# Second half of a transformer layer on TensorE: the up product by seven products over half of its depth

## The chip, the cores and the metric

The kernel runs on one core of a Trainium2 chip. The metric is the device time of one execution in microseconds (us); lower is better. The engines are TensorE (PE), VectorE (DVE), ScalarE (ACT), GpSimd (POOL) and SyncE (SP), which here issues transfers only. They run side by side and wait for one another on semaphores.

## The reference

One layer for 1024 prompt tokens and 64 sample tokens (1088 columns in all), everything in fp32. Width 1024, D_FF 4096. The change lies in the last two lines of the layer:

```
x = x + merged @ w_out
f = rmsnorm(x, norm2_w) @ w_up              # (tokens, 1024) @ (1024, 4096)
x = x + jnp.square(jax.nn.relu(f)) @ w_down  # (tokens, 4096) @ (4096, 1024)
```

A final RMSNorm follows. Ahead of it lie the input projection, a gated convolution, attention for both token groups, and two projections; they are the same in both kernels.

## The kernel before

**Products in three parts.** To keep fp32 accuracy with fp32r matmuls, every operand is split into a high part (a cast to fp32r) and a low part (the operand less its high part). A product is three matmuls into one bank of PSUM: high by high, high by low, low by high (`product`, line 1301). A matmul takes a 128 x 128 stationary tile and up to 512 moving columns.

**Normalised activations.** After the output projection, blocks of 128 tokens are normalised, turned on PE (event `turn_y`, line 1684), and written as `yh` (ScalarE, line 1931) and `yl` (VectorE, line 2312): eight depth tiles (128 rows of the depth 1024) by 1088 columns.

**Twins.** D_FF is worked through in 16 twins; twin n holds the up tiles 2n and 2n+1, each 128 of the 4096 rows. For each up tile, three chunks of columns (384, 384 and 320) are computed, 8 depth tiles by 3 matmuls each (event `up`). VectorE takes relu into `hf`, ScalarE squares it in place. GpSimd splits each up tile's weights (`tail_tile`: cast at line 1229, subtraction at line 1232).

**Seven products down.** The down product of a twin, a 256-deep product for 1024 tokens and 1024 outputs, is already done by the Strassen-Winograd scheme: seven products of half the size (event `prod`, lines 1641 to 1643: 7 x 12 matmuls of 512 columns), with sums of activations on VectorE (event `sum`, line 2335), their high parts on ScalarE and low parts on VectorE (event `prep`, lines 1953 and 2343), and sums of weights (`tw`) with their split on GpSimd (`down_op`, lines 1247 to 1261). The results are added onto `x1` by VectorE (`add_pair`, line 2269). The sample tokens go apart in 8 matmuls (event `few`, lines 1652 and 1653).

**What sets the order.** It is written out by hand: the list `tail` (from line 722) names events, and every engine walks the same list and does its share. For twin n from 1 to 15 it is: sums of twin n-1, six `up` chunks of twin n with `relu` and one or two `prep` of twin n-1 beside each, then the seven `prod` and two `few` of twin n-1. GpSimd has an order of its own: for each twin, five down operands, an up tile, three down operands, an up tile. Down operands go through a ring of five places (`d_hi`, `d_lo`); an operand waits until the one five before it has been used for the last time. At the end, the last twin's down product is done plainly in blocks with the final norm, and GpSimd makes its operands between the last down operands (`end_low`).

## Time and profile before

| | us |
|---|---|
| three runs | 1613.03, 1613.94, 1614.47 |
| median | 1613.94 |
| the profiled execution | 1613.12 |
| its span | 1611.4 |
| up and down stage, from the first up matmul to the last down product | 884.0 to 1581 |

The profiled execution's time is 1.7 us above its span, which runs from the first to the last instruction. PE is busy for 1600.1 us of it, VectorE for 1057.3, GpSimd for 725.1 and ScalarE for 533.8.

A row of a timeline gives start, duration, engine, line of the kernel, operation, output and inputs, shape, count, and in brackets the idle time ahead and what ended it. Matmuls overlap in the array: a duration there is longer than the distance to the next start, and the distance is what PE spends. A row of groups gives after the bar the busy time and the mean in ns of one, then the idle time ahead.

### The profile page before, as it was taken

To read this page: it belongs to the slowest core of one execution; us is meant where nothing else is said; L and a number is where in the kernel's file an instruction comes from. 1 tells how busy PE (TensorE), PEld (TensorE's weight loads), DVE (VectorE), ACT (ScalarE), POOL (GpSimd) and SP (SyncE) were. 2 spreads that over 40 slices of the span, in tenths; PEclk is the share of its full clock that TensorE was granted. 3 is DMA by queue.
4 is the path that set the end of the run, shared out by engine and by line. 5 is a ranking of instruction groups with operands and counts; after the bars stand their busy time and mean duration, and the time that the engine had idled before them with its cause. 6 is when DMAs were issued, how large, how long until landed. Compare 5 with 4: busy or idle time off the path is not lost.

```text
span 1611.4 us, 25421 instructions
## 1 busy us (share of the span) xinstructions
PE 1600.1 (99%) x9776; PEld 1482.7 (92%) x9776; DVE 1057.3 (66%) x1408; ACT 533.8 (33%) x1047; POOL 725.1 (45%) x597
## 2 busy tenths in 40 slices
PE   9999999999999999999999999999999999999998
PEld 8999999999998888999988989999999999999996
DVE  7685877859712221356433588777778888877777
ACT  6655665556522221432134411111111111111124
POOL 5212121121212111223587486666666776666653
PEclk9999999999999999999999999999999999999999
DMA  4201112011184767372354111110111111111012
GB/s 165 68 27 55 54 40 69 27 41 55 41 281 149 234 222 231 117 244 96 129 186 144 58 53 52 53 42 16 49 53 53 52 53 53 53 53 51 18 51 111
DMA packets 133491, 144.99 MB, mean 90 GB/s; under 512 B 7839, under 2 KB 98619, under 8 KB 133372
## 3 DMA queue, kind: packets, MB, share of 16 engines
...
q14 instruction: 41, 0.34, 0.1%
q10 hardware_dynamic: 146, 0.04, 0.0%
...
## 4 chain that ended last, share of the span: by engine, by line
PE 87%; DVE 8%; ACT 3%; issue 1%; DVEq 0%; ACTq 0%
PE ps L1307 51%; PE ps L1641 6%; PE ps L1642 6%; PE ps L1643 6%; DVE sp L2140 2%; PE ps L1598 2%; PE ps L1603 2%; PE ps L1601 2%; PE ps L1501 2%; DVE zc L2132 1%; PE ps L1457 1%; PE ps L1467 1%; PE ps L1545 1%; PE ps L1513 1%; ACT sp L1815 1%
## 5 line engine op out<-in xcount | busy, mean ns | idle before, releaser
L1307 PE MATMUL ps<-xh,wh 128*128 128x352 f32 (+1 forms) x956 | 322.3, 337 | 0.9 <-DVE xl L2113 0.7
L1307 PE MATMUL ps<-xh,wl 128*128 128x352 f32 (+1 forms) x956 | 312.5, 327 | 0.0
L1307 PE MATMUL ps<-xl,wh 128*128 128x352 f32 (+1 forms) x956 | 312.2, 327 | 0.0
L2269 DVE TENSOR_TENSOR x<-ps,x 128x1024 f32<-128x1024 f32 x210 | 257.1, 1225 | 42.9 <-PE ps L1643 24.5
L1150 POOL CAST wh<-raw 128x1024 fp32r<-128x1024 f32 x48 | 50.4, 1050 | 477.6 <-issue 213.2
L1307 PE MATMUL ps<-yh,wh 128*128 128x384 f32 (+1 forms) x768 | 250.5, 326 | 0.0
L1307 PE MATMUL ps<-yh,wl 128*128 128x384 f32 (+1 forms) x768 | 250.5, 326 | 0.0
L1307 PE MATMUL ps<-yl,wh 128*128 128x384 f32 (+1 forms) x768 | 250.2, 326 | 0.0
L1939 ACT ACTIVATE hf<-hf 128x384 f32<-128x384 f32 (+1 forms) x96 | 48.6, 508 | 554.9 <-DVE hf L2322 554.9
L1307 PEld LDWEIGHTS ps<-xh,wh 128*128 128x128 f32 x956 | 179.8, 188 | 17.2 <-issue 15.5
L1307 PEld LDWEIGHTS ps<-xl,wh 128*128 128x128 f32 x956 | 180.0, 188 | 0.7
L1307 PEld LDWEIGHTS ps<-xh,wl 128*128 128x128 f32 x956 | 179.5, 188 | 0.0
L1641 PE MATMUL ps<-d_hi,a_hi 128*128 128x512 f32 x420 | 163.7, 390 | 0.3 <-DVE x L2257 0.3
L1643 PE MATMUL ps<-d_lo,a_hi 128*128 128x512 f32 x420 | 163.7, 390 | 0.0
L1642 PE MATMUL ps<-d_hi,a_lo 128*128 128x512 f32 x420 | 163.7, 390 | 0.0
L1159 POOL TENSOR_TENSOR wl<-raw,wh 128x1024 fp32r<-128x1024 f32 x48 | 116.2, 2420 | 97.0 <-DVE zc L2142 91.2
L1307 PEld LDWEIGHTS ps<-yh,wh 128*128 128x128 f32 x768 | 144.2, 188 | 0.7 <-POOL wl L1232 0.2
L1307 PEld LDWEIGHTS ps<-yl,wh 128*128 128x128 f32 x768 | 144.2, 188 | 0.5
L1307 PEld LDWEIGHTS ps<-yh,wl 128*128 128x128 f32 x768 | 144.1, 188 | 0.0
L1232 POOL TENSOR_TENSOR wl<-raw,wh 128x1024 fp32r<-128x1024 f32 x56 | 135.5, 2420 | 10.1 <-POOL wh L1229 10.1
L1259 POOL CAST d_hi<-raw_d 128x512 fp32r<-128x512 f32 x60 | 37.5, 624 | 166.0 <-PE ps L1653 141.6
L2184 DVE COPY kct<-ps 128x512 f32<-128x512 f32 x32 | 22.1, 692 | 128.2 <-PE ps L1501 103.8
...
## 6 DMA issues: line engine op xcount, KB each, us to landing
...
```

The costliest lines, as they stand in the source:

```text
L1150: g.tensor_copy(wh[s][:, :], raw[s][:, :]).then_inc(w_hi, 1)
L1159: g.tensor_tensor(wl[s][:, :], raw[s][:, :], f32(wh[s][:, :]), ALU.subtract).then_inc(w_split, 1)
L1232: g.tensor_tensor(low[:, :], raw[n % 3][:, :], f32(high[:, :]), ALU.subtract).then_inc(w_split, 1)
L1259: g.tensor_copy(high, src).then_inc(d_hi, 1)
L1307: ins = mm(out, lhs[:, k * P:(k + 1) * P], rhs[:, x], start=(first and a == 0 and m == 0), stop=(last and a == n - 1 and m == 2))
L1501: ins = tr(bank(tb, p * P, (p + 1) * P), cache[g][:, (a * NPAIR + p) * P:(a * NPAIR + p + 1) * P], ident[:, :])
L1598: mm(out, hi, w, start=k == 0, stop=False)
L1641: mm(out, a_hi[p][:, x], w, start=not onto, stop=False, skip_group_check=onto)
L1642: mm(out, a_lo[p][:, x], w, start=False, stop=False, skip_group_check=onto)
L1643: ins = mm(out, a_hi[p][:, x], lo_w, start=False, stop=True, skip_group_check=onto)
L1939: A(x, x, ACT.Square).then_inc(hf_made, 1)
L2269: V_.tensor_tensor(x, src, x, ALU.add).then_inc(step_free, 1)
```

## The change

The up product of twins 1 to 15 is done in another way. Its output is two up tiles (i = 0, 1) by two halves of the prompt tokens (j = 0, 1), its depth eight tiles. The first four depth tiles are done by seven products in the Strassen-Winograd scheme, the last four plainly.

- PE does eight entries `mix` per twin: seven products of 6 matmuls (two depth tiles by three), and four plain sums of 12 matmuls, which share the entries (`MIX`: bank, product, plain part). All have 512 columns: 90 matmuls. Four banks hold partial sums that the scheme uses more than once; PE goes on adding onto a bank once a copy has been kept.
- ScalarE copies such partial sums into `hf` (`keep`), VectorE adds them to another bank (`join`), ScalarE does relu and square, which were one instruction on each.
- The 64 sample tokens have 16 matmuls of 256 columns with the weights as moving side, a copy (`few_move`) and a ninth entry of two small matmuls in plain fp32 that turn and add their high and low parts.
- The weights of a twin are one buffer `raw_u` (two loads of 4 depth tiles). Six operands are made of it: four plain ones of two depth tiles, whose cast is on ScalarE (`u_cast`) and whose subtraction is on GpSimd, and two of sums (`twist` on 256 columns), with cast and subtraction on GpSimd. They share the ring of five places with the eight down operands; places are handed out by who is free first.
- GpSimd's order per twin is six up operands, then eight down operands.
- In the first twin (still plain), the activations lie in other buffers, so the second and third chunks are cut in pieces at columns 512 and 1024; VectorE writes plain copies `y_plain` in `turn_y`, and VectorE and ScalarE make four sums of them (`twist`, `twist_low`) during its last chunks.

The core of the diff:

```diff
+        MIX_BANK = {"x": 4, "y": 5, "z": 6, "w": 0, "few": 1}
+        MIX = [("x", 0, None), ("y", 1, (0, 0)), ("z", 3, None), ("x", 2, None), ("z", 5, (0, 1)), ("x", 4, None), ("w", 6, (1, 0)),
+               ("x", None, (1, 1))]
+        KEEP = {0: (0, 0), 2: (1, 1), 3: (0, 1), 5: (1, 0)}
+        JOIN = {1: (0, 0), 4: (0, 1), 6: (1, 0), 7: (1, 1)}
+        U_KT = (0, 4, 6, 2)
+        PLAIN_AT = {f: (x, (f - U_KT[x]) * 2 * P) for x in range(4) for f in (U_KT[x], U_KT[x] + 1)}
+        W_AT = {p: [(PLAIN_AT[f][0], PLAIN_AT[f][1] + i * P) for f in fs] for p, i, fs in ((0, 0, (0, 1)), (1, 0, (2, 3)), (6, 1, (2, 3)))}
+        W_AT.update({p: [(x, (KQ * h + q) * P) for q in range(KQ)] for p, x, h in ((3, 4, 0), (2, 4, 1), (5, 5, 0), (4, 5, 1))})
+        U_LAST = (1, 7, 7, 6, 3, 5)
...
         for n in range(1, N_TWIN):
-            tail += [("sum", n - 1, k) for k in range(4)]
-            todo = list(PREP)
-            for m in range(6):
-                e = 2 * n + m // 3, m % 3
-                tail += [("up", *e), ("relu", *e)]
-                for _ in range(BESIDE_UP[m]):
-                    tail.append(("prep", n - 1, todo.pop(0)))
-            assert not todo
+            m = n - 1
+            if n == 1:
+                tail += [("u_cast", n, x) for x in range(4)]
+            tail += [("sum", m, 0), ("sum", m, 1), ("mix", n, 0), ("keep", n, 0), ("prep", m, 0), ("prep", m, "few0"), ("prep", m, "few1"),
+                     ("prep", m, 1), ("prep", m, 6), ("prep", m, 3), ("prep", m, 4), ("mix", n, 1), ("few_move", n), ("sum", m, 2),
+                     ("mix", n, 2), ("keep", n, 2), ("mix", n, 3), ("keep", n, 3), ("prep", m, 2), ("join", n, 1), ("sum", m, 3),
+                     ("mix", n, 4), ("mix", n, 8), ("prep", m, 5), ("mix", n, 5), ("keep", n, 5), ("join", n, 4), ("join", n, 8),
+                     ("mix", n, 6), ("join", n, 6), ("mix", n, 7), ("join", n, 7)]
             if n == LAST_TWIN:
                 tail.append(("end_prep",))
             tail += [("prod", n - 1, 0), ("few", n - 1, 0)]
             tail += [("prod", n - 1, p) for p in range(1, N_WAY)]
+            if n < LAST_TWIN:
+                tail += [("u_cast", n + 1, x) for x in range(3)]
             tail.append(("few", n - 1, 1))
+            if n < LAST_TWIN:
+                tail.append(("u_cast", n + 1, 3))
...
+        RING = []
+        for n in range(1, N_TWIN):
+            RING += [("u", n, x) for x in range(len(U_LAST))]
+            RING += [("d", n - 1, k) for k in range(N_OP)]
+        ring_no = {e: g for g, e in enumerate(RING)}
+
         def op_used(g):
 
-            n, k = divmod(g, N_OP)
-            return done_no[(OP_LAST[k][0], n, *OP_LAST[k][1:])]
+            kind, n, k = RING[g]
+            return done_no["mix", n, U_LAST[k]] if kind == "u" else done_no[(OP_LAST[k][0], n, *OP_LAST[k][1:])]
+
+        slot_of, slot_after = [], []
+        free_at = [tile_end["up", 0], tile_end["up", 0], tile_end["up", 1], tile_end["up", 1], tile_end["up", 1] + 1]
+        for g in range(len(RING)):
+            slot_of.append(free_at.index(min(free_at)))
+            slot_after.append(min(free_at))
+            free_at[slot_of[g]] = op_used(g)
...
+            def load_pair(n):
+
+                if n == 1:
+                    sp_.wait_ge(w_split, 6 * NPAIR + 3 * KT + 2 + N_OUT + 2)
+                else:
+                    sp_.wait_ge(d_lo, ring_no["u", n - 1, len(U_LAST) - 1] + 1)
+                apart(sp_)
+                for s in range(2):
+                    sp_.dma_start(blocks(raw_u, 2 * P)[:, 4 * s:4 * s + 4, :], wup[:, 4 * s:4 * s + 4, ds(2 * n * P, 2 * P)]).then_inc(u_in, 16)
...
+            def slot_free(of):
+
+                pool.wait_ge(step_done, slot_after[of])
+                if of == TOP_FIRST:
+                    pool.wait_ge(twist_lo, 4)
+                apart(pool)
+
+            def split_op(of, src):
+
+                high, low = w_hi_at[slot_of[of]][:, :], w_lo_at[slot_of[of]][:, :]
+                kind, n, x = RING[of]
+                if kind == "u" and x < 4:
+                    pool.wait_ge(u_hi, 4 * (n - 1) + x + 1)
+                else:
+                    g.tensor_copy(high, src).then_inc(d_hi, 1)
+                    pool.wait_ge(d_hi, of + 1 - 4 * n if kind == "u" else of + 1 - 4 * (n + 1))
+                g.tensor_tensor(low, src, f32(high), ALU.subtract).then_inc(d_lo, 1)
+                pool.wait_ge(d_lo, of + 1)
+
+            def up_op(n, x):
+
+                rows_ = blocks(raw_u, 2 * P)
+                a11, a12, a21, a22 = (rows_[:, KQ * j:KQ * j + KQ, i * P:i * P + P] for i in range(2) for j in range(2))
+                s1, s2, s4, s3 = (blocks(tw[t])[:, KQ * h:KQ * h + KQ, :] for t in range(2) for h in range(2))
+                of = ring_no["u", n, x]
+                if x == 0:
+                    pool.wait_ge(u_in, 32 * n)
+                if x < 4:
+                    slot_free(of)
+                    split_op(of, raw_u[:, U_KT[x] * 2 * P:(U_KT[x] + 2) * 2 * P])
+                elif x == 4:
+                    twist(s1, a21, a22, ALU.add)
+                    twist(s2, s1, a11, ALU.subtract)
+                    slot_free(of)
+                    split_op(of, tw[0][:, :])
+                else:
+                    twist(s3, a11, a21, ALU.subtract)
+                    twist(s4, a12, s2, ALU.subtract)
+                    slot_free(of)
+                    split_op(of, tw[1][:, :])
...
+                for x in range(len(U_LAST)):
+                    up_op(n + 1, x)
+                for k in range(N_OP):
+                    if n == LAST_TWIN - 1 and k >= N_SOON:
                         end_low(k - N_SOON)
                     down_op(n, k)
...
+                    if m < len(MIX):
+                        where, p, over = MIX[m]
+                        out = bank(MIX_BANK[where])
+                        if m in (3, 4, 5, 7):
+                            pe.wait_ge(kept, 4 * (n - 1) + KEPT_FOR[m])
+                        else:
+                            pe.wait_ge(step_free, mix_bank_read(n, m))
+                        begun = where == "x" and m > 0 or (where == "z" and m > 2)
+                        if over:
+                            i, j = over
+                            for f in range(KT // 2, KT):
+                                x, at = PLAIN_AT[f]
+                                pe.wait_ge(d_lo, ring_no["u", n, x] + 1)
+                                ins = three(out, weight(x, at + i * P), [y_at(f, part, j * HS, (j + 1) * HS) for part in range(2)],
+                                            not begun and f == KT // 2, p is None and f == KT - 1)
+                            begun = True
+                        if p is not None:
+                            pe.wait_ge(d_lo, ring_no["u", n, W_AT[p][0][0]] + 1)
+                            if n == 1 and p in TWIST_NO:
+                                pe.wait_ge(twist_lo, TWIST_NO[p] + 1)
+                            for q in range(KQ):
+                                ins = three(out, weight(*W_AT[p][q]), [y_op[p][part][:, q * HS:(q + 1) * HS] for part in range(2)],
+                                            not begun and q == 0, q == KQ - 1)
+                        if m == 1:
+                            pe.wait_ge(d_lo, ring_no["u", n, 3] + 1)
+                            order_ = [f for x in (1, 2, 3, 0) for f in (U_KT[x], U_KT[x] + 1)]
+                            for f in order_:
+                                x, at = PLAIN_AT[f]
+                                y = y_few[f // (KT // 2)][:, f % (KT // 2) * P:f % (KT // 2) * P + P]
+                                for t, w in enumerate((w_hi_at, w_lo_at)):
+                                    ins = mm(bank(MIX_BANK["few"], 0, 2 * P), y, w[ring("u", n, x)][:, at:at + 2 * P],
+                                             start=f == order_[0] and t == 0, stop=f == order_[-1] and t == 1)
...
+                elif e[0] == "twist":
+                    act.wait_ge(step_done, tile_end["up", 0])
+                    for k, p in enumerate(TWIST_OF):
+                        if k == 3:
+                            act.wait_ge(step_done, tile_end["up", 1])
+                        act.wait_ge(twisted, k + 1)
+                        A(y_op[p][0][:, :], y_plain[TWIST_IN[k]][:, :], ACT.Copy).then_inc(twist_hi, 1)
...
+                elif e[0] == "u_cast":
+                    _, n, x = e
+                    of = ring_no["u", n, x]
+                    act.wait_ge(u_in, 32 * n)
+                    act.wait_ge(step_done, slot_after[of])
+                    assert of != TOP_FIRST
+                    A(w_hi_at[slot_of[of]][:, :], raw_u[:, U_KT[x] * 2 * P:(U_KT[x] + 2) * 2 * P], ACT.Copy).then_inc(u_hi, 1)
...
+                elif e[0] == "keep":
+                    _, n, m = e
+                    i, j = KEEP[m]
+                    if n >= 2 and m == 0:
+                        act.wait_ge(op_lo, len(PREP) * (n - 1))
+                    act.wait_ge(step_done, done_no["mix", n, m])
+                    A(hf[n % 2][i][:, j * HS:(j + 1) * HS], bank(MIX_BANK[MIX[m][0]]), ACT.Copy).then_inc(kept, 1)
+                elif e[0] == "join":
+                    _, n, m = e
+                    act.wait_ge(step_free, read_no["mix", n, m])
+                    parts = [hf[n % 2][JOIN[m][0]][:, JOIN[m][1] * HS:(JOIN[m][1] + 1) * HS]] if m < 8 else [hf[n % 2][i][:, SEQ:NTOK] for i in range(2)]
+                    for x in parts:
+                        if m < 8:
+                            A(x, x, ACT.Relu).then_inc(relu_made, 1)
+                            act.wait_ge(relu_made, 4 * (n - 1) + RELU_NO[m])
+                        A(x, x, ACT.Square).then_inc(hf_made, 1)
...
+                        if f < KT // 2 and b < NB:
+                            x = (f % KQ) * HS + b * P % HS
+                            V_.tensor_scalar(y_plain[f // KQ, b * P // HS][:, x:x + P], src, w2c[:, f:f + 1], None, ALU.mult)
...
+                elif e[0] == "join":
+                    _, n, m = e
+                    v.wait_ge(step_done, done_no["mix", n, m])
+                    if m < 8:
+                        i, j = JOIN[m]
+                        x = hf[n % 2][i][:, j * HS:(j + 1) * HS]
+                        v.wait_ge(kept, 4 * (n - 1) + 1 + [KEEP[k] for k in (0, 2, 3, 5)].index(JOIN[m]))
+                        V_.tensor_tensor(x, bank(MIX_BANK[MIX[m][0]]), x, ALU.add).then_inc(step_free, 1)
```

On GpSimd (POOL), around the beginning of a steady twin, the order before was (`raw` and `wh`, `wl`: an up tile and its parts; `raw_d`: down weights, `tw`: their sums, `d_hi`, `d_lo`: places of the ring):

```order
L1229 CAST wh_61<-raw_59 128x1024 [waits step_done,d_lo,raw_in0]
L1232 TENSOR_TENSOR wl_63<-raw_59,wh_61 128x1024 [waits w_hi]
L1259 CAST d_hi_116<-raw_d_127 128x512 [waits step_done]
L1261 TENSOR_TENSOR d_lo_121<-raw_d_127,d_hi_116 128x512 [waits d_hi]
L1255 TENSOR_TENSOR tw_129<-raw_d_127,tw_129 128x512 [waits d_lo,step_done]
L1259 CAST d_hi_117<-tw_129 128x512 [waits t_made]
L1261 TENSOR_TENSOR d_lo_122<-tw_129,d_hi_117 128x512 [waits d_hi]
L1259 CAST d_hi_118<-raw_d_126 128x512 [waits d_lo,step_done]
L1261 TENSOR_TENSOR d_lo_123<-raw_d_126,d_hi_118 128x512 [waits d_hi]
L1229 CAST wh_62<-raw_60 128x1024 [waits step_done,d_lo,raw_in1]
L1232 TENSOR_TENSOR wl_64<-raw_60,wh_62 128x1024 [waits w_hi]
```

and is now, from the subtraction of the first up operand of a twin to the second operand of sums:

```order
L1344 TENSOR_TENSOR d_lo_149<-raw_u,d_hi_144 128x512 [waits step_done,d_lo,u_in,u_hi]
L1344 TENSOR_TENSOR d_lo_150<-raw_u,d_hi_145 128x512 [waits d_lo,step_done,u_hi]
L1344 TENSOR_TENSOR d_lo_148<-raw_u,d_hi_143 128x512 [waits d_lo,step_done,u_hi]
L1344 TENSOR_TENSOR d_lo_151<-raw_u,d_hi_146 128x512 [waits d_lo,step_done,u_hi]
L1324 TENSOR_TENSOR tw_138<-raw_u 128x256 [waits d_lo]
L1324 TENSOR_TENSOR tw_138<-tw_138,raw_u 128x256 [waits t_made]
L1342 CAST d_hi_147<-tw_138 128x512 [waits t_made,step_done]
L1344 TENSOR_TENSOR d_lo_152<-tw_138,d_hi_147 128x512 [waits d_hi]
L1324 TENSOR_TENSOR tw_139<-raw_u 128x256 [waits d_lo]
L1324 TENSOR_TENSOR tw_139<-raw_u,tw_138 128x256 [waits t_made]
L1342 CAST d_hi_144<-tw_139 128x512 [waits t_made,step_done]
L1344 TENSOR_TENSOR d_lo_149<-tw_139,d_hi_144 128x512 [waits d_hi]
```

All splits of up weights now stand in one run ahead of the down operands, in pieces of 512 columns; the third subtraction waits (through its cast) for the last of the seven products of the twin before, the fourth and the cast of the first sum operand for the `few` behind it.

On ScalarE (ACT), where the first twin ends and twin 1 begins, the order is now (`y_plain` to `yh`: casts of the four sums of activations; `hf<-hf`: squares of the first twin; `d_hi<-raw_u`: casts of up weights; the last row is the first kept copy):

```order
L2122 ACTIVATE yh_97<-y_plain_105 128x1024 [waits twisted,step_done]
L2122 ACTIVATE yh_101<-y_plain_107 128x1024 [waits twisted]
L2122 ACTIVATE yh_99<-y_plain_108 128x1024 [waits twisted]
L2122 ACTIVATE yh_103<-y_plain_106 128x1024 [waits twisted,step_done]
L2115 ACTIVATE hf_1_135<-hf_1_135 128x320 [waits step_free]
L2115 ACTIVATE hf_0_134<-hf_0_134 128x384 [waits step_free]
L2115 ACTIVATE hf_1_135<-hf_1_135 128x384 [waits step_free]
L2129 ACTIVATE d_hi_143<-raw_u 128x512 [waits step_done,u_in]
L2129 ACTIVATE d_hi_144<-raw_u 128x512 [waits step_done,u_in]
L2129 ACTIVATE d_hi_145<-raw_u 128x512 [waits step_done,u_in]
L2129 ACTIVATE d_hi_146<-raw_u 128x512 [waits step_done,u_in]
L2142 ACTIVATE hf_0_136<-ps 128x512 [waits step_done]
```

Before, only the squares stood there. The fourth cast waits for the last matmul of the first twin, and the casts of weights stand behind it.

## Rows read from the trace of the kernel before

**Rows 1.** The page: PE's busy time, and the clock in 40 slices.
```profile
PE 1600.1 (99%) x9776; PEld 1482.7 (92%) x9776; DVE 1057.3 (66%) x1408; ACT 533.8 (33%) x1047; POOL 725.1 (45%) x597
...
PEclk9999999999999999999999999999999999999999
```

**Rows 2.** Timeline of PE: end of a twin, up part, down products, next twin.
```profile
1045.09 0.39 PE L1653 MATMUL ps<-d_lo,few 128*128 128x512 f32 x1
1045.32 0.33 PE L1307 MATMUL ps<-yh,wh 128*128 128x384 f32 x1
...
1069.04 0.39 PE L1641 MATMUL ps<-d_hi,a_hi 128*128 128x512 f32 x1
...
1089.95 0.33 PE L1307 MATMUL ps<-yh,wh 128*128 128x384 f32 x1
```

**Rows 3.** Timeline of PE in the attention stage: matmuls of 256, 128, 64 columns.
```profile
241.57 0.28 PE L1484 MATMUL ps<-tl,vhl 128*128 128x256 f32 x1
241.69 0.22 PE L1483 MATMUL ps<-th,vhl 128*128 128x128 f32 x1
241.75 0.28 PE L1484 MATMUL ps<-tl,vhl 128*128 128x128 f32 x1
...
487.62 0.43 PE L1520 MATMUL ps<-ks,qblk 128*32 128x64 f32 x16
```

**Rows 4.** Groups by line: the first from the page, the others of the last stages.
```profile
L1232 POOL TENSOR_TENSOR wl<-raw,wh 128x1024 fp32r<-128x1024 f32 x56 | 135.5, 2420 | 10.1 <-POOL wh L1229 10.1
...
L1261 POOL TENSOR_TENSOR d_lo<-raw_d,d_hi 128x512 fp32r<-128x512 f32 x60 | 78.0, 1300 | 4.8
...
L1259 POOL CAST d_hi<-raw_d 128x512 fp32r<-128x512 f32 x60 | 37.5, 624 | 166.0 <-PE ps L1653 141.6 <-DMA raw_d<-in_w_down 13.2 <-PE ps L1643 5.6
...
L1953 ACT ACTIVATE a_hi<-sum 128x512 fp32r<-128x512 f32 x60 | 35.5, 615 | 0.0
L1939 ACT ACTIVATE hf<-hf 128x384 f32<-128x384 f32 x64 | 33.6, 526 | 502.4 <-DVE hf L2322 502.4
...
L1961 ACT ACTIVATE end_wh<-end_raw 128x1024 fp32r<-128x1024 f32 x2 | 2.0, 1051 | 1.7 <-DMA end_raw<-in_w_down 1.7
```

**Rows 5.** Timeline of GpSimd and VectorE where the same twin begins.
```profile
1047.44 1.62 POOL L1249 TENSOR_TENSOR tw<-raw_d,tw 128x512 f32<-128x512 f32 x1
...
1045.75 0.68 DVE L2257 TENSOR_TENSOR x<-ps,x 128x512 f32<-128x512 f32 x1
1046.35 1.56 DVE L2335 TENSOR_TENSOR sum<-hf,hf 128x512 f32<-128x512 f32 x1
...
1062.57 0.68 DVE L2343 TENSOR_TENSOR a_lo<-sum,a_hi 128x512 fp32r<-128x512 f32 x1
```

**Rows 6.** Timeline of PE and VectorE: last chunks of the first twin.
```profile
902.41 0.34 PE L1307 MATMUL ps<-yh,wh 128*128 128x384 f32 x1
...
910.73 0.33 PE L1307 MATMUL ps<-yh,wh 128*128 128x384 f32 x1
...
900.27 2.16 DVE L2312 SCALAR_TENSOR_TENSOR yl<-ps,cols,yh 128x128 fp32r<-128x128 f32 x8 [1.98 <-ACT yh L1931]
```

**Rows 7.** Timeline of GpSimd and PE: last down products.
```profile
1562.52 2.42 POOL L1268 TENSOR_TENSOR end_l<-hf,end_h 128x1024 fp32r<-128x1024 f32 x1 [13.68 <-ACT end_h L1958]
...
1578.17 1.30 POOL L1261 TENSOR_TENSOR d_lo<-raw_d,d_hi 128x512 fp32r<-128x512 f32 x1
...
1559.95 0.39 PE L1641 MATMUL ps<-d_hi,a_hi 128*128 128x512 f32 x1
...
1579.94 0.39 PE L1652 MATMUL ps<-d_hi,few 128*128 128x512 f32 x1
```

**Rows 8.** Timeline of PE in the first down products.
```profile
940.05 0.50 PE L1641 MATMUL ps<-d_hi,a_hi 128*128 128x512 f32 x1 [0.30 <-DVE x L2257]
```

**Rows 9.** Windows at the span's end: length, busy times, then the clock.
```profile
1605.00:1607.50 2.50, 0.00 (x0) 0.00 (x0) 2.43 (x6) 1.67 (x4) 0.00 (x0) 1.00 0.34 143
1607.50:1609.00 1.50, 0.00 (x0) 0.00 (x0) 0.83 (x2) 0.00 (x0) 0.00 (x0) 0.62 1.01 415
```

263 lines of the change are left out of this document (169 added, 94 removed).

## The prediction

> **What bounds the kernel now.** I read the page first, for which engine is full. TensorE is busy in 99% of the span, its clock is at full level in every slice [rows 1]. Nothing but work on PE can be worth much, and any new wait of PE is paid in full. I then read PE's timeline over one twin in steady state, for where such a twin begins and ends. From the first matmul of its up part to the first of the down products are 23.72 us, and from there to the next twin 20.91 us [rows 2]. That is 144 and 92 matmuls, one after the other without a hole; the 92 matmuls of 512 columns go at 0.2273 us each, the chunks of 384 columns at 0.1733 (48 of them in 8.32 us [rows 6]). There are fifteen such twins, 44.63 us each. The other engines have to be ahead of PE, no more. Last I read GpSimd and VectorE in the same twin, for what their instructions cost alone and beside each other [rows 4, 5], because the change gives both a longer list ahead of PE.
>
> **1. The arithmetic of a twin.** The 144 matmuls go. In their place stand 90 of 512 columns: seven products of 6, and four plain sums of 12. By 0.2273 that is 20.46 us. The 64 sample tokens go apart, as 16 matmuls of 256 columns. A 256-column matmul lies 0.12 us before the next [rows 3]: 1.92 us. The two small matmuls with plain fp32 operands are four passes. Sixteen such passes over 32 weight columns fit in 0.43 us [rows 3], under 0.03 each; a 256-column pass is 0.12. So four cost between 0.1 and 0.5 us; I take 0.45, for they load all 128 columns and PE drains between kinds. Together 22.83 against 23.72: **0.89 us less, times 15: -13.4 us** (-12.7 to -18.6). The saved sixteenth of the product is smaller than it sounds because the gain of wide chunks is partly spent on the sample tokens.
>
> **2. The fifth operand, in every steady twin.** The third entry of a twin (product 3) needs the operand of sums s1 and s2. Its place in the ring is free only when the last matmul of the twin before is done, and so is that of the operand before it. The chain from there, at time 0: a waiting engine starts 0.43 us later (VectorE's add at 1045.75, PE having gone on at 1045.32 [rows 2, 5]); ScalarE's cast 0.6; GpSimd's subtraction 1.3 and 0.2 to the next; two sums of 256 columns, 0.73 each (estimate from 1.30 for 512 and 2.42 for 1024 columns), a cast 0.62, a subtraction 1.30 [rows 4]; 0.1 for each of five hand-overs. Sum 6.4. PE wants it after 24 matmuls of 512 and 16 of 256, at 7.4. Alone it would be in time by 1.0 us. But VectorE does its two sums and three low parts just then. Where it meets GpSimd both wait: a sum began at 1046.35 and took 1.56 us, against 0.68 for the same work at 1062.57, and GpSimd's subtraction beside it 1.62 against 1.30 [rows 4, 5]. So each of the five adds some 0.3 to the chain, 1.5 in all: ready at 7.9, **0.45 us late, 14 times: +6.3 us**. The lower bound is no wait (interference under 1.0), the upper that each adds its own whole length, three of 0.68 and two of 0.23, and starts ahead: 1.45 late, +20.3. I take the value near the measured rows. The Trainium skill (SBUF — State Buffer, the shared port pair) says that the pair is locked for a whole instruction and the loser blocks fully; by that alone the sum would be the upper bound, while the rows show a growth of 0.32 for GpSimd.
>
> **3. The start.** At the end of the first twin, PE now finds no operand. Before, GpSimd split the next tiles meanwhile and PE went straight on at 910.73 [rows 6]. Now ScalarE stands in the order: cast of the fourth twist (waits for that last matmul), three squares, then the casts for twin 1. From the last matmul: 0.43, 1.05, 3 x 0.45 (squares chained), 0.6 and 0.1, that is 3.5 [rows 4]. GpSimd then does four subtractions (1.3 + 0.2 each, 6.0), two sums (1.6), a cast (0.7), a subtraction (1.3): 12.9 to 13.1, plus six meetings with VectorE of 0.3: 14.9. PE's own work up to product 3 is 7.4. **+7.6 us** (5.8 with no meeting, 9.9 with whole lengths), of which some 5 lie ahead of twin 1 and the rest in it. The load of up weights for twin 1 waits for a split that ends around the first chunk of the first twin, so it costs nothing; the down weights' load waits for the last twist but is used 20 us later.
>
> **4. The first twin in pieces.** Two chunks out of three are cut at columns 512 and 1024: 36 more matmuls for each tile. A 128-column one follows at 0.06 us [rows 3], a 64-column one costs no less than a third of that and no more than the same. So 24 extra of 64 columns cost 0.3 to 1.0, 12 of 128 0.2; per tile 0.85, twice: 1.7. VectorE also writes a plain copy: four more instructions of about 0.27 for the last block [rows 6], and the chunk waits for all of it: 0.6. **+2.3 us** (1.0 to 3.5). The same copies in the output projection lie under PE work of 4 us a tile and cost nothing; were they late there, each of eight blocks would show its 1 us.
>
> **5. The end.** In the last twin GpSimd's run of end splits is already the tightest: it starts at 1562.52, ends with the split of 1578.17 (1.30 us), and PE uses that at 1579.94, 20.0 us after its products began at 1559.95 [rows 7]. The chain of 17.0 us keeps its length. But two down operands that were made early now wait for ring places that the up part frees at its very end, and stand ahead of it: 0.43 + 2.1 + 1.5 + 2.1, so it starts 6.3 us after the products' start, ends at 23.3. **+3.4 us** (2.4 to 4.0), and all behind it follows.
>
> **6. What goes.** A 0.3 us wait of the first down products on VectorE [rows 8], whose sums GpSimd then slowed: **-0.3**. ScalarE's casts, copies and squares (some 25 of 0.6 in 44) have room. The copy that the last plain sum waits for stands behind a high part that waits for VectorE's sum; by the same steps it is done 2.8 us early, so it costs nothing unless VectorE falls behind by that.
>
> Sum: -13.4 + 6.3 + 7.6 + 2.3 + 3.4 - 0.3 = +5.9. The profiled execution took 1613.12, which gives 1619.0. The median of the runs is 0.8 above it, so the forecast is **1619.5 us**.
>
> **Rivals.** *GpSimd is in time in every steady twin.* Decides: interference under 1.0 us instead of 1.5, so if VectorE's small low parts slip through. Then term 2 is nothing: 1613.2, no change; with the lower ends of terms 1, 3, 4 and 5 too (-2 to -5 for the small matmuls, -1.8, -1.3, -1.0) it is 1607 to 1609, faster. For it: only 1.0 us has to be found, and GpSimd's ordinary subtractions average 1.30 even beside VectorE [rows 4]. Against: the sums stand exactly there. *The lock counts in full*, which is the rule cited above: 1.45 us per twin, 1633. *The clock falls at the start.* After its last matmul, in the profile's last microseconds, PE stood still; the clock was full in 1605 to 1607.5 and lower in the next stretch [rows 9], 1.2 instead of 2.4 GHz. PE will stand still some 5 us here. At half clock the 7.4 us up to product 3 become 14.8, of which 2.6 fit into its wait: 0 to 5 us, 1622. The Trainium skill (TensorE: Matmul & The Clock Gate, HAM oscillation) warns of such holes before matmuls. *VectorE and ScalarE trail*: the last kept copy comes 1 us late in each twin, 1634. That the seven products save nothing is excluded by the count.
>
> **Chances.** Forecast 0.40, in time 0.36, full lock 0.13, clock 0.07, trailing 0.04. A measurement of this kernel tells 0.2%, 3.2 us, from no change: 1610.7 to 1617.2 around the median. Of the forecast 0.07 falls in there, of the rival in time 0.16, its other 0.20 below. So faster 0.20, same 0.23, slower 0.57. The likeliest case alone has 1614 to 1625. The range of 1607 to 1630 leaves out 0.05 below and 0.13 above.
>
> **What would show it.** In the changed profile: about 22.8 us of PE work between products plus a hole of some 0.5 us ahead of product 3 that GpSimd's low part of a twist ends; a hole of about 5 us after the first twin, ended by GpSimd, and more before product 3; one of 3 us before the last sample-token product. If the hole before product 3 is missing in the steady twins, term 2 is wrong and the kernel is no slower. If holes stand before the last plain sum instead, ScalarE's queue is the fault.

## The result and the profile after

| | before | after |
|---|---|---|
| median of four runs | 1613.9 | 1634.73 |
| range | 1613.03 to 1614.47 | 1633.04 to 1635.15 |
| the profiled execution | 1613.12 | 1633.04 |
| its span | 1611.4 | 1631.3 |

The changed kernel is **1.3% slower**: the ratio is 1.0128, with a 95% interval of 1.0110 to 1.0145. The forecast was 1619.5, its range ended at 1630. The side was right, the size was not. Between the two profiled spans lie 19.9 us, between the two medians 20.8.

The page and the waits of PE come first, as before the change. The columns of the waits are: what waited and for what; us in total, times, longest.

```profile
PE 1599.0 (98%) x9338; PEld 1425.3 (87%) x9338; DVE 1040.3 (64%) x1448; ACT 649.4 (40%) x1246; POOL 819.3 (50%) x718
...
PE ps L1828 <- POOL d_lo L1344: 17.9, 15, 4.3
PE ps L1773 <- POOL d_lo L1344: 3.5, 1, 3.5
```

PE has 438 matmuls less than in [rows 1] and is busy for 1.1 us less. Against that stand sixteen waits that were not there, 21.4 us in all. Each is ended by GpSimd: one in each of the fifteen twins, and one at the end.

**The steady twin.** PE's timeline, with the first row of each part (compare [rows 2]); then GpSimd and VectorE in the same twin, and ScalarE's two casts. The product in question is product 3, the third entry.

```profile
1056.57 0.39 PE L1828 MATMUL ps<-yh,d_hi 128*128 128x512 f32 x1
...
1062.01 0.28 PE L1866 MATMUL ps<-d_hi,y_few 128*128 128x256 f32 x1
...
1065.04 0.47 PE L1828 MATMUL ps<-yh,d_hi 128*128 128x512 f32 x1 [0.97 <-POOL d_lo L1344]
...
1080.60 0.39 PE L1763 MATMUL ps<-d_hi,a_hi 128*128 128x512 f32 x1
...
1101.47 0.39 PE L1828 MATMUL ps<-yh,d_hi 128*128 128x512 f32 x1
```

```profile
1056.63 1.30 POOL L1344 TENSOR_TENSOR d_lo<-raw_u,d_hi 128x512 fp32r<-128x512 f32 x1 [3.11 <-ACT d_hi L2129]
1058.14 1.50 POOL L1344 TENSOR_TENSOR d_lo<-raw_u,d_hi 128x512 fp32r<-128x512 f32 x1 [0.20 <-PE ps L1828]
1059.72 1.07 POOL L1324 TENSOR_TENSOR tw<-raw_u 128x256 f32<-128x256 f32 x1
1060.87 1.07 POOL L1324 TENSOR_TENSOR tw<-tw,raw_u 128x256 f32<-128x256 f32 x1
1062.13 1.10 POOL L1342 CAST d_hi<-tw 128x512 fp32r<-128x512 f32 x1 [0.19 <-POOL tw L1324]
1063.30 1.59 POOL L1344 TENSOR_TENSOR d_lo<-tw,d_hi 128x512 fp32r<-128x512 f32 x1
...
1057.60 0.88 DVE L2579 TENSOR_TENSOR sum<-hf,hf 128x512 f32<-128x512 f32 x1
1058.41 1.78 DVE L2579 TENSOR_TENSOR sum<-hf 128x512 f32<-128x512 f32 x1
1060.11 1.22 DVE L2587 TENSOR_TENSOR a_lo<-hf,a_hi 128x512 fp32r<-128x512 f32 x1
...
1062.08 0.68 DVE L2587 TENSOR_TENSOR a_lo<-hf,a_hi 128x512 fp32r<-128x512 f32 x1
...
1062.68 1.09 DVE L2587 TENSOR_TENSOR a_lo<-hf,a_hi 128x512 fp32r<-128x512 f32 x1
...
1055.92 0.63 ACT L2129 ACTIVATE d_hi<-raw_u 128x512 fp32r<-128x512 f32 x1 [4.81 <-PE ps L1765]
1056.83 0.63 ACT L2129 ACTIVATE d_hi<-raw_u 128x512 fp32r<-128x512 f32 x1 [0.28 <-PE ps L1774]
```

The up part lasts 24.03 us here and the twin 44.90, against 23.72 and 44.63. The sixteen matmuls of 256 columns end at 1063.90 (1.89 us after 1062.01), and PE goes on at 1065.04: a hole of 1.14, and the first matmul behind it takes 0.09 more than its 0.23. Without these 1.23 us the twin would take 43.67, less than before. The operand was due 7.33 us after the twin's start and was finished at 8.32. GpSimd began with the fourth operand at 1.57, because the third, whose ring place came free only with the seventh down product, was still under way. And every one of its five instructions is longer than its length alone: VectorE is at work beside each.

**The start.** The end of the first twin and the start of the next, on PE, ScalarE and GpSimd; then windows (length, PE busy, clock, DMA share, GB/s).

```profile
915.90 0.28 PE L1819 MATMUL ps<-yh,wl 128*128 128x256 f32 x1
920.47 0.76 PE L1828 MATMUL ps<-yh,d_hi 128*128 128x512 f32 x1 [4.29 <-POOL d_lo L1344]
...
917.18 1.28 ACT L2115 ACTIVATE hf<-hf 128x320 f32<-128x320 f32 x3
918.37 2.17 ACT L2129 ACTIVATE d_hi<-raw_u 128x512 fp32r<-128x512 f32 x4
...
919.06 1.26 POOL L1344 TENSOR_TENSOR d_lo<-raw_u,d_hi 128x512 fp32r<-128x512 f32 x1 [30.89 <-ACT d_hi L2129]
...
928.03 1.62 POOL L1344 TENSOR_TENSOR d_lo<-tw,d_hi 128x512 fp32r<-128x512 f32 x1
```

```profile
915.90:920.40 4.50, 0.28 (x3) 0.84 0.15 35
920.40:924.00 3.60, 3.53 (x8) 0.50 0.64 248
```

PE stood still for 4.3 us. ScalarE's cast of the fourth twist (from 916.22) and its three squares stand ahead of the first cast of weights, and GpSimd begins when that is done. From 918.9 to 925.7 the clock was at its lower level, 1.2 GHz: the 24 matmuls of the first two entries took 8.05 us instead of 5.44. Product 3 began at 930.41, and did not wait, for its operand was ready at 929.65. The first up part and its down products took 50.8 us, 7.1 more than PE's own 43.67.

**The end.** PE behind its last down product, and one window.

```profile
1598.16 0.73 PE L1773 MATMUL ps<-d_hi,few 128*128 128x512 f32 x1 [3.47 <-POOL d_lo L1344]
...
1599.96 0.63 PE L1789 MATMUL ps<-end_wh,end_h 128*128 128x512 f32 x1
```

```profile
1598.00:1603.00 5.00, 4.84 (x14) 0.66 0.02 3
```

The hole is followed by the lower clock again, from 1598.2 to 1601.6; the four matmuls behind it took 1.80 us instead of 0.91. From the first of these products to the first block it is 25.4 us against 20.9 before, and the blocks behind took 0.8 more.

**The first twin** took 32.0 us instead of 26.8. The chunk with the sample tokens went from 3.6 to 5.5 us:

```profile
890.49 0.28 PE L1819 MATMUL ps<-yh_rest,wl 128*128 128x256 f32 x1
890.61 0.31 PE L1819 MATMUL ps<-y_few,wh 128*128 128x64 f32 x2
...
890.86 0.36 PE L1819 MATMUL ps<-yh_rest,wh 128*128 128x256 f32 x1
```

So the 19.9 us are: first twin 5.2, twin 1 5.5, the other up parts 3.9, the end 4.5 and 0.8.

### The profile page after: what moved, and what is told of

Its sections match the earlier page's. It is cut to its first block, busy times and chain, and to the rows that moved or that the text cites. A ratio compares the mean times of both kernels' runs of the same rounds, so it can differ in the third digit from the quotient of the medians.

```text
span 1631.3 us, 25154 instructions
## 1 busy us (share of the span) xinstructions
PE 1599.0 (98%) x9338; PEld 1425.3 (87%) x9338; DVE 1040.3 (64%) x1448; ACT 649.4 (40%) x1246; POOL 819.3 (50%) x718
## 3 DMA queue, kind: packets, MB, share of 16 engines
q8 instruction: 75, 1.23, 0.3%
## 4 chain that ended last, share of the span: by engine, by line
PE 82%; DVE 7%; POOL 6%; ACT 3%; issue 2%; DVEq 0%; POOLq 0%; ACTq 0%
PE ps L1429 29%; PE ps L1828 16%; PE ps L1764 6%; PE ps L1765 6%; PE ps L1763 6%; POOL d_lo L1344 3%; DVE sp L2352 2%; PE ps L1720 2%; PE ps L1725 2%; POOL tw L1324 2%; PE ps L1723 2%; PE ps L1623 2%; PE ps L1819 2%; DVE zc L2344 1%; PE ps L1579 1%
## 5 line engine op out<-in xcount | busy, mean ns | idle before, releaser
L1245 POOL TENSOR_TENSOR wl<-raw,wh 128x1024 fp32r<-128x1024 f32 x48 | 116.2, 2420 | 97.0 <-DVE zc L2354 91.2
L2129 ACT ACTIVATE d_hi<-raw_u 128x512 fp32r<-128x512 f32 x60 | 37.6, 631 | 238.2 <-PE ps L1765 234.4
L1344 POOL TENSOR_TENSOR d_lo<-raw_u,d_hi 128x512 fp32r<-128x512 f32 x60 | 80.8, 1347 | 87.3 <-ACT d_hi L2129 77.9
L1344 POOL TENSOR_TENSOR d_lo<-tw,d_hi 128x512 fp32r<-128x512 f32 x90 | 120.9, 1343 | 7.2
L1828 PE MATMUL ps<-yh,d_hi 128*128 128x512 f32 x210 | 84.9, 404 | 17.9 <-POOL d_lo L1344 17.9
L2352 DVE TENSOR_TENSOR_SCAN sp<-sp 128x1024 f32<-128x1024 f32 (+3 forms) x64 | 88.4, 1382 | 17.0 <-ACT sp L1994 16.9
L2557 DVE TENSOR_TENSOR hf<-ps,hf 128x512 f32<-128x512 f32 x60 | 41.2, 686 | 89.3 <-PE ps L1828 89.3
L2587 DVE TENSOR_TENSOR a_lo<-sum,a_hi 128x512 fp32r<-128x512 f32 x60 | 67.4, 1142 | 42.0 <-ACT a_hi L2165 42.0
L1828 PE MATMUL ps<-yh_rest,d_hi 128*128 128x512 f32 x240 | 94.1, 392 | 0.0
L1828 PE MATMUL ps<-yh_rest,d_lo 128*128 128x512 f32 x240 | 93.9, 391 | 0.0
```

What stands on the lines that cost most here:

```text
L1245: g.tensor_tensor(wl[s][:, :], raw[s][:, :], f32(wh[s][:, :]), ALU.subtract).then_inc(w_split, 1)
L1344: g.tensor_tensor(low, src, f32(high), ALU.subtract).then_inc(d_lo, 1)
L1828: ins = mm(out, w[high], y[part], start=start and t == 0, stop=stop and t == 2, skip_group_check=True)
L2352: V_.tensor_tensor_scan(rev, rev, rev, 0.0, ALU.add, ALU.bypass).then_inc(suffix_made, 1)
L2557: V_.tensor_tensor(x, bank(MIX_BANK[MIX[m][0]]), x, ALU.add).then_inc(step_free, 1)
L2587: V_.tensor_tensor(a_lo[x][:, :], op_source(n, x), f32(a_hi[x][:, :]), ALU.subtract).then_inc(op_lo, 1)
```

## The experiments

All are edits of the changed kernel. They were compared with the kernel before on the same chip, whose median there was between 1613.65 and 1613.76. The changed kernel was not timed again beside them: differences from it go by its median of 1634.73, and by the profiled executions where the text says so.

### e1: the sums made in idle time

```
+                if x == 2:
+                    twist(s1, a21, a22, ALU.add)
+                    twist(s2, s1, a11, ALU.subtract)
                 if x < 4:
                     slot_free(of)
...
                 elif x == 4:
-                    twist(s1, a21, a22, ALU.add)
-                    twist(s2, s1, a11, ALU.subtract)
                     slot_free(of)
```

> GpSimd makes s1 and s2 already after the first two subtractions of a twin, in the 3.1 us in which it stood idle; no work is added or left out. Theory A (GpSimd's chain behind the end of the twin before is too long by its own sum of terms): the chain loses two sums of 1.07 and a hand-over, its low part is ready about 2.2 us earlier, at 6.1 after the start of the twin where product 3 wants it at 7.3. The hole of 1.14 us ahead of product 3 goes in the 14 steady twins, 16 us: 1618.7 us. Start and end stay (a hole of 4.3 us after the first twin, one of 3.5 before the last sample product). Theory B (what holds the kernel is VectorE and ScalarE, which trail behind the kept copies): the hole moves to a later product, the cycle stays at 44.90 and the time within 3 us of 1634.7. Theory C (contention for the port in full): the sums in the idle time are free as well, but the rest of the chain, still beside VectorE, grows so that 0.3 to 0.5 us of the hole is left: 1623 to 1626.

Measured: 1617.29 us (1616.52 to 1618.21), ratio to before 1.0022 (1.0013 to 1.0032), 17.4 us less than the changed kernel. The first of GpSimd's two sums and the end of its row, then PE:

```profile
1052.10 0.74 POOL L1324 TENSOR_TENSOR tw<-raw_u 128x256 f32<-128x256 f32 x1
...
1058.79 1.62 POOL L1344 TENSOR_TENSOR d_lo<-tw,d_hi 128x512 fp32r<-128x512 f32 x1
...
1061.83 0.28 PE L1867 MATMUL ps<-d_lo,y_few 128*128 128x256 f32 x1
1061.95 0.40 PE L1829 MATMUL ps<-yh,d_hi 128*128 128x512 f32 x1
```

The hole is gone in the steady twins and no other has taken its place: the up part takes 22.80 us. A is borne out, within 1.5 us; B and C are not. PE waits for neither VectorE nor ScalarE in these twins, and two instructions that were lengthened by 0.3 each are no longer on the chain.

### e2: VectorE out of GpSimd's way

```
-            tail += [("sum", m, 0), ("sum", m, 1), ("mix", n, 0), ("keep", n, 0), ("prep", m, 0), ("prep", m, "few0"), ("prep", m, "few1"),
-                     ("prep", m, 1), ("prep", m, 6), ("prep", m, 3), ("prep", m, 4), ("mix", n, 1), ("few_move", n), ("sum", m, 2),
-                     ("mix", n, 2), ("keep", n, 2), ("mix", n, 3), ("keep", n, 3), ("prep", m, 2), ("join", n, 1), ("sum", m, 3),
+            tail += [("mix", n, 0), ("keep", n, 0), ("mix", n, 1), ("few_move", n), ("mix", n, 2), ("keep", n, 2),
+                     ("join", n, 1), ("sum", m, 0), ("sum", m, 1), ("prep", m, 0), ("prep", m, "few0"), ("prep", m, "few1"),
+                     ("prep", m, 1), ("prep", m, 6), ("prep", m, 3), ("prep", m, 4), ("sum", m, 2),
+                     ("mix", n, 3), ("keep", n, 3), ("prep", m, 2), ("sum", m, 3),
```

> VectorE's and ScalarE's work on the down operands of a twin (two sums, seven high and low parts) is moved behind the first joined product, so that VectorE is quiet while GpSimd makes the operands up to that of product 3; no work is added or left out. Theory A (the meetings with VectorE lengthen GpSimd's chain by some 1.7 us): the sums of 256 columns take 0.73 instead of 1.07, the cast 0.6 instead of 1.10, the subtraction 1.3 instead of 1.6; the operand is ready at 6.6 to 6.8 instead of 8.3 and the hole ahead of product 3 is gone: 16 us less, 1619, unless the operands of the down products, now made in the last 5 us of the up part, are late: then a hole of up to 2 us stands ahead of the down products in its place. Theory B (GpSimd is that slow by itself, these are the lengths of the instructions): the lengths and the hole of 1.14 stay, 1635.

Measured: 1662.9 us (1661.65 to 1664.49), ratio 1.0308. GpSimd in the twin that begins at 1061.59, and PE's new hole in it:

```profile
1063.16 1.29 POOL L1345 TENSOR_TENSOR d_lo<-raw_u,d_hi 128x512 fp32r<-128x512 f32 x1 [0.20 <-PE ps L1829]
1064.53 0.73 POOL L1325 TENSOR_TENSOR tw<-raw_u 128x256 f32<-128x256 f32 x1
1065.34 0.74 POOL L1325 TENSOR_TENSOR tw<-tw,raw_u 128x256 f32<-128x256 f32 x1
1066.27 0.61 POOL L1343 CAST d_hi<-tw 128x512 fp32r<-128x512 f32 x1 [0.19 <-POOL tw L1325]
1066.96 1.29 POOL L1345 TENSOR_TENSOR d_lo<-tw,d_hi 128x512 fp32r<-128x512 f32 x1
...
1083.70 0.50 PE L1829 MATMUL ps<-yh_rest,d_hi 128*128 128x512 f32 x1 [1.86 <-ACT hf L2143]
```

Two things follow. The lengths are those of A: 1.29, 0.73, 0.74, 0.61 and 1.29, together 4.66, where the changed kernel has 1.50, 1.07, 1.07, 1.10 and 1.59, together 6.33. **VectorE's presence costs this chain 1.67 us**, and without it the operand is ready 6.66 after the twin's start, in time by 0.7. The same instruction starts at +1.57 in both kernels, so that lag is not VectorE's doing. But the time became worse, not better. The hole that I had expected ahead of the down products stands ahead of the last plain sum, and ScalarE ends it: its copy of the fourth kept partial sum is queued behind high parts that wait for VectorE. This is the rival "VectorE and ScalarE trail", brought about by the edit. The twin takes 45.9 us, and in nine of them some 1.6 more, because the clock falls behind the hole of 1.9 us (0.72 in the window from 1036 to 1042, 1.00 from 1012 to 1036). Fourteen times 0.97 and nine times 1.6 make 28.0 of the 28.6 us by which its span is longer than the changed kernel's.

### e3 and e6: the start

The first attempt moved the four casts for twin 1 on ScalarE ahead of the fourth cast of a twist. The second also put two of them ahead of all four, and changed VectorE's row and PE's wait:

```
-                        if k == 3:
-                            act.wait_ge(step_done, tile_end["up", 1])
+                        if k in (0, 3):
+                            for x in ((0, 1), (2, 3))[k // 3]:
+                                u_cast(1, x)
...
-                 ("up", 1, 1), ("relu", 0, 1), ("twist_low", 2), ("relu", 1, 1), ("twist_low", 3)]
+                 ("up", 1, 1), ("relu", 0, 1), ("relu", 1, 1), ("twist_low", 2), ("twist_low", 3)]
...
             if n == 1:
-                return read_no["up", 1, 1]
+                return read_no["up", int(m > 0), 1]
```

> ScalarE makes the casts for twin 1 ahead of its cast of the fourth twist and of the squares, two of them before the last chunk of the first twin; no work is added or left out. Theory A (the hole of 4.3 us after the first twin is the queue of ScalarE, and the half clock follows from the hole): no hole there, matmuls 0.227 apart at once, and product 3 waits 0.5 to 1.5 us as in the steady twins. The first cycle takes 44.9 to 45.4 us instead of 50.8: 5.4 to 5.9 less, 1629 us. Theory B (the clock falls there for another reason, such as the kind of products that begin): the hole goes but the first 24 matmuls still take some 8 us instead of 5.45: 3 us less at most. Theory C (GpSimd's four subtractions hold it): the hole is split in pieces between the products, and under 2 us are won.

> The start once more, with VectorE's and ScalarE's rows both put right: ScalarE makes two casts for twin 1 ahead of all casts of the twists and two right behind the last matmul; VectorE reads the last bank of the first twin ahead of its third low part of a twist; the first product no longer waits for that bank, which it does not write. No work is added or left out. Theory A (rows of other engines, late by their order): a hole under 0.6 us after the first twin, no fall of the clock; product 3 waits 1 to 1.5 us as in the steady twins. From the last matmul of the first twin to the second cycle 45.2 to 46 us instead of 50.8 in the changed kernel and 48.3 with the first attempt: 5 to 5.5 us less than the changed kernel, 1629.3. Theory B (the four long subtractions of VectorE, 1.2 to 2.1 us each, hold GpSimd's in full wherever they stand): two of GpSimd's first four subtractions take 2 us or more, product 3 waits over 2 us, and the gain is under 4 us.

Measured: e3 1631.13 us (1630.97 to 1631.27), ratio 1.0108; e6 1629.69 (1627.64 to 1630.11), ratio 1.0096. PE's first matmul of twin 1 and that of product 3, in e3 and then in e6:

```profile
918.17 0.50 PE L1828 MATMUL ps<-yh,d_hi 128*128 128x512 f32 x1 [1.63 <-DVE hf L2542]
...
928.22 0.47 PE L1828 MATMUL ps<-yh,d_hi 128*128 128x512 f32 x1 [1.74 <-issue]
```

```profile
918.51 0.51 PE L1828 MATMUL ps<-yh,d_hi 128*128 128x512 f32 x1 [1.39 <-DVE hf L2542]
...
927.07 0.47 PE L1828 MATMUL ps<-yh,d_hi 128*128 128x512 f32 x1 [0.95 <-issue]
```

The rows with "issue" name no releaser; GpSimd's low part for product 3 ended 0.1 us ahead of each of them, at 928.12 and 926.97. The hole of 4.3 us was ScalarE's queue, as A of e3 says, and the low clock went with the hole: with 1.6 us of it the clock stayed at 1.00 from 915 to 926. B of e3 falls. But the hole did not vanish. In e3 part of it stood ahead of product 3 (1.7 us), as C has it, though more than C's 2 us was won. The rest stood ahead of the first product. VectorE ended that one, late with its read of the first twin's last bank; putting that row right gave only 0.2 us more there, because VectorE's low parts of 1024 columns and GpSimd's subtractions lengthen one another (2.0 and 2.3 us instead of 1.30 on GpSimd in e6). The first cycle is 46.7 us in e6 from the last matmul of the first twin to the next cycle, against 50.8 in the changed kernel, 48.4 in e3 and 45.2 to 46 expected: 4.2 us less. The medians differ by 5.0. A of e6 holds for the clock, and B names what is left, but neither came out in its numbers: the hole was 1.4 us where A had under 0.6, and product 3 waited about 1 us where B had over 2.

### e4: the pieces of the first twin

```
+                    runs = [(f, piece) for f in order_ for piece in y_pieces(f, a, z)]
+                    runs.sort(key=lambda r: r[1][0] - r[1][1])
+                    for f, piece in runs:
...
```

> In the first twin the matmuls of a chunk are sorted by width, so that the 24 of 64 columns stand together behind the 24 of 256, and 256 before 128; the same matmuls, only their order changes. Theory A (a narrow matmul between wide ones costs because the next weights' load finds no cover): the 24 of 256 go back to 0.12 each and the 24 of 64, together, cost between 0.03 and 0.08: the chunk of both takes 3.6 to 4.8 us instead of 5.5, and the first twin 2 to 4 us less. Theory B (each matmul costs its columns or one load of weights of about 0.11, whichever is longer): 24 x 0.12 and 24 x 0.11, the chunk stays at 5.5 us, with 0.11 between the narrow ones, and the time stays within 0.5 us.

Measured: one run, 1633.95 us, and the chunk took 5.56. Weight loads (PEld) across the border from 256 to 64 columns:

```profile
892.82 0.19 PEld L1819 LDWEIGHTS ps<-yh,wh 128*128 128x128 f32 x1
892.94 0.19 PEld L1819 LDWEIGHTS ps<-yl,wh 128*128 128x128 f32 x1
...
893.18 0.31 PEld L1819 LDWEIGHTS ps<-y_few,wh 128*128 128x128 f32 x2
893.41 0.19 PEld L1819 LDWEIGHTS ps<-y_few,wl 128*128 128x128 f32 x1
```

B is right, on this one run. The 24 of 256 columns took 2.96 us (0.123 each), the 24 of 64 columns 2.60 (0.108 each), and twelve of 128 columns 1.29 (0.1075 each). Beside matmuls of 64, 128 and 256 columns alike, a weight load of 128 columns stands 0.11 to 0.12 after the one before. In a run of such matmuls none was cheaper. The Trainium skill (TensorE: Matmul & The Clock Gate, LDWEIGHTS) gives the time of a load in ns as the number of weight columns over 1.2, which is 107 ns for 128, and these runs agree.

### e5: the end

ScalarE makes the high parts of the sixth and eighth down operand of the last twin (new event `d_cast`), and GpSimd's second split of end weights comes last:

```
-                tail.append(("end_prep",))
+                tail += [("end_prep",), ("d_cast", 5), ("d_cast", 7)]
...
-                    for s in range(2):
+                    for s in (k - 2,):
                         pool.wait_ge(end_w_hi, s + 1)
...
+                if n == LAST_TWIN - 1:
+                    end_low(3)
```

> In the last twin ScalarE, which stands idle there for 19 us, makes the high parts of the sixth and eighth down operand, and GpSimd makes the last low part ahead of the second of its two splits of the end weights (2.36 us) instead of behind both; no work is added or left out. Theory A (GpSimd's row of subtractions behind the up part sets the end): the eighth operand is ready some 3 us earlier, the hole of 3.5 us ahead of the last two sample products shrinks to 0.5 to 1 us, the second end weight then costs up to 0.7 us ahead of the first block, and the clock does not fall, which gives back 0.9 us on four matmuls and 0.8 in the blocks: 3.5 to 4.5 us less in all, 1630.5. Theory B (the clock falls at the end in any case): the holes shrink as said and 1.7 us less is won, 1632.

Measured: 1629.91 us (1629.13 to 1630.28), ratio 1.0100, 4.8 less. PE's first sample product and the one wait that is left:

```profile
1596.16 0.47 PE L1778 MATMUL ps<-d_hi,few 128*128 128x512 f32 x1
...
1598.54 0.50 PE L1794 MATMUL ps<-end_wh,end_h 128*128 128x512 f32 x1 [0.52 <-POOL end_wl L1399]
```

The hole ahead of the sample products is gone, a wait of 0.5 stands in the first block (0.9 from one start to the next), and the four matmuls take 1.01 us: the clock holds. A is right, a little better than expected.

### e8: the casts back on GpSimd

```
-                if kind == "u" and x < 4:
-                    pool.wait_ge(u_hi, 4 * (n - 1) + x + 1)
-                else:
-                    g.tensor_copy(high, src).then_inc(d_hi, 1)
...
+                g.tensor_copy(high, src).then_inc(d_hi, 1)
+                pool.wait_ge(d_hi, of + 1)
```

> One part of the change undone: the four plain high parts of a twin's up weights are made by GpSimd again, ahead of each subtraction, instead of by ScalarE. No work is left out. Theory A (the chain on GpSimd decides, and the casts on ScalarE are what kept the hole small): for the fourth operand a cast of 0.6 to 0.9 and a hand-over come into the chain, the hole ahead of product 3 grows from 1.14 to 1.9 to 2.3 us, 14 times 0.8 to 1.2: 11 to 16 us more, 1646 to 1651, and up to 10 us more where the clock falls for it. Theory B (GpSimd would have waited for ScalarE's cast as long as its own takes): no difference, 1635.

Measured: 1638.1 us (1637.34 to 1639.14), ratio 1.0150: 3.4 more than the changed kernel, between the two theories and far less than I expected. In the steady twin the hole ahead of product 3 grew only from 1.14 to 1.35, and 0.2 us came in the two entries ahead of it, so the cycle takes 45.36 instead of 44.90. GpSimd no longer waits for ScalarE's answer: it begins the third operand's cast itself as soon as the place is free, and that subtraction ends 1.40 us after the twin's start, against 1.36. At the start it is better by 1.7 us, for the casts do not stand behind ScalarE's squares. The part "casts on ScalarE" is worth 0.46 us a twin, 6.4 in all, less what it costs at the start.

### e7 and e9: the repairs together

e7 holds e1, e6 and e5. e9 also has GpSimd make s1 and s2 of twin 1 ahead of its first ring place, and VectorE read each of the first twin's last two banks as soon as it is full.

> The three repairs together: s1 and s2 made in GpSimd's idle time, the start in its second order, the end with two casts on ScalarE. No work is left out. If the holes are the whole difference, their gains add: 17.4 (measured alone), 5 to 5.5, 3.5 to 4.5, and the hole ahead of product 3 in twin 1, which is in none of them, another 1. From 1634.7 that is 1606 to 1609, faster than the kernel before by 5 to 8 us: cycles of 43.7 us, 14 of them 12.9 us less than before, against 3.3 us more in the first twin and some 1.5 at start and end each. If instead VectorE or ScalarE trails once GpSimd is early, new holes stand ahead of the joined products, and it stays at 1612 or above.

> The three repairs together, with the start in a third order: GpSimd makes s1 and s2 of twin 1 while it waits for the first free ring place (it stood idle there for 24 us), and VectorE reads the last two banks of the first twin each as soon as it is full, ahead of its low parts of the twists. No work is added or left out. Theory A (what is left at the start are two rows: VectorE's, 1.67 us between the last matmul of the first twin and the next, and GpSimd's, 0.95 us inside the first two products): the first gap becomes 0.3 us, GpSimd's third subtraction starts at once instead of behind two sums of 1.6 and 0.7, and the first cycle is 1.5 to 2.5 us shorter than with the second order: 1606.6 to 1607.6. Theory B (GpSimd's subtractions, 2.0 to 2.3 us each beside VectorE's 1024-wide ones, hold PE all the same): what is won ahead of the first product is lost ahead of product 3, and the time stays within 0.7 us of 1609.1.

Measured: e7 1609.12 us (1608.49 to 1609.39), ratio 0.9971 (0.9961 to 0.9982); e9 **1607.61 us** (1607.27 to 1608.27), ratio 0.9964 (0.9950 to 0.9977). Both are faster than the kernel before. In e9 PE goes on at once behind the first twin, and two waits of note are left in twin 1:

```profile
917.20 0.40 PE L1836 MATMUL ps<-yh,d_hi 128*128 128x512 f32 x1
...
922.52 0.50 PE L1836 MATMUL ps<-yh,d_hi 128*128 128x512 f32 x1 [0.57 <-POOL d_lo L1347]
...
926.64 0.47 PE L1836 MATMUL ps<-yh,d_hi 128*128 128x512 f32 x1 [0.55 <-issue]
```

e7 is 25.6 us below the changed kernel. Measured alone, the three gave 17.4, 5.0 and 4.8, and the wait of product 3 in twin 1 another 1: they add up to 28.2, of which 2.6 are missing. The first cycle shows about half of that: 46.8 us in e7, no shorter than in e6, since the early sums of twin 1 stand ahead of GpSimd's third subtraction. In e9 it is 46.0. Much of the rest is not in this stage at all. From the first up matmul to the span's end the profiled executions took 747.4 us (changed kernel), 730.4 (e1), 743.5 (e6), 743.4 (e5) and 722.2 (e7): gains of 17.0, 3.9 and 4.0, with the 1 together 25.9, against 25.2. So only 0.7 is missing there; the medians differ by more because executions of one kernel do (1633.04 to 1635.15 for the changed kernel, whose profiled one is the fastest). So the holes were the difference, and what is left is PE's arithmetic, up parts of 22.80 us against 23.72, less the 5.2 us that the first twin costs in pieces and what remains of start and end.

## Why the prediction was wrong

The forecast's sum was +5.9, the spans differ by 19.9. By its own terms:

1. **Arithmetic of a twin, -0.89: right.** PE's own up part is 22.80 us in e1, against 22.83 forecast. The four passes of the two small matmuls took 0.36 (0.45 forecast), the sixteen of 256 columns 1.89 (1.92). The forecast explained part of its 0.45 by a drain of PE between kinds of matmuls. No run shows a drain; what shows is that the second matmul behind the small ones starts 0.32 us after the first instead of 0.23, and with this 0.09 the sum closes: 20.46 + 1.89 + 0.36 + 0.09 = 22.80.
2. **The fifth operand, +0.45 a twin: the step that failed.** It is 1.23 a twin, a hole of 1.14 and a slower matmul behind it. Forecast and measured steps stand side by side:

| from the twin's start | forecast | measured |
|---|---|---|
| GpSimd begins the fourth operand | 1.13 | 1.57 |
| its five instructions alone | 4.68 | 4.66 (e2) |
| VectorE beside them | 1.5 | 1.67 |
| hand-overs, up to PE's start | 0.6 | 0.57 |
| PE goes on | 7.9 | 8.47 |
| PE could have gone on | 7.45 | 7.33 |

   What I left out is the third operand. I let the chain begin with the end of the twin before, on an idle GpSimd. But that operand's place comes free only at the end of the seventh down product, 0.9 us earlier; with ScalarE's reaction and cast and 1.3 of subtraction GpSimd is occupied until +1.36. That is the largest part of the miss, 0.44, although ScalarE's reaction was 0.26 where the forecast had 0.43; the rest is the interference (0.17) and the earlier need (0.12). The hole is 0.69 us longer than forecast, and 0.09 come behind it: fourteen times 0.78, 10.9 of the 14.0 missing. The interference was forecast at 0.3 a meeting, and the bound with whole instructions, three of 0.68 and two of 0.23, at 2.5; measured 1.67. The trace says what a meeting costs. Take from the end of each GpSimd instruction its length alone (e2), and one has the time at which it could have begun its work; beside it, the end of the VectorE instruction that was under way:

| GpSimd | starts | end less length alone | VectorE's instruction ends |
|---|---|---|---|
| fourth subtraction | 1058.14 | 1058.35 | 1058.48 |
| first sum | 1059.72 | 1060.06 | 1060.19 |
| second sum | 1060.87 | 1061.20 | 1061.33 |
| cast | 1062.13 | 1062.62 | 1062.76 |
| subtraction | 1063.30 | 1063.60 | 1063.77 |

   The two agree to 0.13 to 0.17 us in every row: GpSimd waits for the rest of the instruction under way, then works at full speed. VectorE does the same in turn: its sum that starts at 1058.41 ends at 1060.19, 0.55 after GpSimd's fourth subtraction (1059.64), while it takes 0.68 alone. So the growth depends on where in VectorE's instruction GpSimd arrives, and the bound with five whole lengths was the forecast's reading, not what the rows show. The Trainium skill (SBUF — State Buffer, SBUF: two separate sides) says that whichever of the two starts first has the shared port pair for its whole instruction and that the other fully blocks; these rows agree with it. That the forecast's bound (1633) came near the measured time was chance, since the third operand is not in it.
3. **The start, +7.6: about right, 7.1.** The wait ahead of twin 1 was 4.3 us (some 5 forecast). What followed was not a second wait but the low clock: it stretched PE's first two entries by 2.6 us, and so product 3 found its operand ready. The rival "the clock falls at the start" came true and cost little more, some 0.6 us: the operand, ready at 929.65, would have held product 3 until about 929.8, and it began at 930.41. That the sum came out near was luck in part: the forecast had the 2.6 us as a wait for GpSimd.
4. **The first twin in pieces, +2.3: too small, 5.2.** From the row 241.69 and the next at 241.75 [rows 3] I took 0.06 for a 128-column matmul and at most as much for one of 64. The row behind that pair starts 0.11 later, and the weight loads there stand 0.11 apart all along (241.58, 241.69, 241.80): a single distance between two starts was no price. 24 of 64 columns cost 1.9 us a tile and not 0.3 to 1.0, 12 of 128 columns 0.7 and not 0.2. The sixteen in 0.43 us that seemed to speak for cheap ones have 32 weight columns. VectorE's plain copies, 0.6 in the forecast, delayed nothing.
5. **The end, +3.4: 5.3.** The hole was 3.5 us; the low clock behind it added 0.9 on four matmuls and 0.8 in the blocks.
6. **-0.3:** the first down products do not wait, as forecast.

The misses are 2.9 in the first twin, -1.2 in twin 1 (+5.5 where terms 1 and 3 made +6.7), 10.4 in the other up parts (+3.9 where terms 1, 2 and 6 made -6.5), and 1.9 at the end: 14.0. The upper bound of term 2 (1.45 us late) was above the measured 1.14, but I gave 0.13 to the case of the full lock and ended the range at 1630, below it. VectorE and ScalarE did not trail; e2 shows how little it takes that they do.
